# Rows that every partition needs, copied through DRAM by broadcast DMA in place of TensorE products, in a two-layer hybrid block with its delta-rule chain one step shorter

## What is computed

```
qkv = silu(conv(x @ w))                      # q, k, v: four heads each
q, k = l2_normalize(q), l2_normalize(k)      # one root per head and token
beta = sigmoid(ba)
g    = -exp(a_log) * softplus(aa + dt_bias)  # one number per head and token
gc   = cumsum(g) within a chunk
decay = exp(gc[i] - gc[j]) for j <= i
T    = inverse(I + strict_lower(beta k k^T * decay))
...                                          # scan over chunks with the state S
S    = S * exp(gc[last]) + (k * exp(gc[last] - gc))^T v_new
o    = rms_norm(o) * silu(z)                 # one root per head and token
```

## Time and profile before

| | us |
|---|---|
| median of 3 runs | 1946.79 (1946.22 to 1951.45) |
| the profiled execution | 1947.63 |
| its span in the profile | 1945.8 |
| PE busy | 1931.6 (99%) |
| DVE, ACT, POOL busy | 1021.6, 888.9, 851.3 |

### The profile page before, as it was taken

One profiled execution on the slowest core, in us unless ns is written; L12 is line 12 of the kernel. 1 busy time (PEld: TensorE's weight loads), 2 busy tenths in 40 slices (PEclk: granted clock), 3 DMA queues, 4 the chain that ended last, 5 costly groups with the idle time before them and its releaser, 6 DMA issues.

```text
span 1945.8 us, 23734 instructions
## 1 busy us (share of the span) xinstructions
PE 1931.6 (99%) x9108; PEld 1532.9 (79%) x9108; DVE 1021.6 (53%) x1832; ACT 888.9 (46%) x1355; POOL 851.3 (44%) x644
## 2 busy tenths in 40 slices
PE   9999999999999999999999999999999999999999
PEld 6878877877788878787877788677766788888887
DVE  5657755555745668666464747574644436101210
ACT  6455553344345455543344355586555444312321
POOL 4545432443445454422434445455322445444443
PEclk9999999999999999999999999999999999999999
DMA  5334542423535235632424545322111332222232
GB/s 202 128 110 135 139 137 73 162 76 118 187 107 175 90 114 147 162 109 71 153 65 141 189 154 162 136 76 98 65 56 55 119 107 89 98 97 98 98 114 71
DMA packets 94864, 227.69 MB, mean 117 GB/s; under 512 B 29880, under 2 KB 32952, under 8 KB 93440
## 3 DMA queue, kind: packets, MB, share of 16 engines
q1 hardware_dynamic: 89056, 223.03, 35.4%
q10 hardware_dynamic: 5696, 3.15, 0.6%
HBM read 194.01 MB, written 24.64 MB: 112 GB/s over the span
## 4 chain that ended last, share of the span: by engine, by line
PE 85%; DVE 7%; DMA 2%; ACT 2%; POOL 1%; SPq 1%; issue 1%; ACTq 0%; DVEq 0%
PE bank L442 84%; DVE ER L376 1%; DVE kv L376 1%; PE bank L446 1%; SPq L371 1%; POOL wl L376 1%; DMA X<-inverses 1%; DMA gt<-gates 1%; DVE scs L401 1%; DMA kv<-blocks 1%; DVE m8s L398 0%; ACT lt L428 0%; DVE lt L386 0%; DVE tmp L376 0%; ACT wh L431 0%
## 5 line engine op out<-in xcount | busy, mean ns | idle before, releaser
L376 POOL TENSOR_TENSOR wl<-st,wh 128x512 fp32r<-128x512 f32 x602 | 804.5, 1359 | 1019.3 <-ACT wh L431 1019.2
L442 PE MATMUL bank<-hh,wh 128*128 128x512 f32 x1616 | 651.8, 404 | 2.8 <-DVE hl L386 0.9
L442 PE MATMUL bank<-hh,wl 128*128 128x512 f32 x1616 | 629.8, 390 | 0.0
L442 PE MATMUL bank<-hl,wh 128*128 128x512 f32 x1616 | 629.3, 390 | 0.0
L431 ACT ACTIVATE wh<-st 128x1024 fp32r<-128x1024 f32 (+1 forms) x302 | 317.0, 1050 | 242.9 <-PE bank L442 194.5
L442 PEld LDWEIGHTS bank<-hh,wh 128*128 128x128 f32 x1616 | 303.4, 188 | 92.5 <-issue 24.6
L442 PEld LDWEIGHTS bank<-hl,wh 128*128 128x128 f32 x1616 | 303.6, 188 | 66.9 <-issue 6.9
L442 PEld LDWEIGHTS bank<-hh,wl 128*128 128x128 f32 x1616 | 303.3, 188 | 64.3
L376 DVE TENSOR_TENSOR xt<-xt,bank 128x512 f32<-128x512 f32 x40 | 27.5, 687 | 235.6 <-PE bank L442 235.6
L428 ACT ACTIVATE tmp<-bank 128x512 f32<-128x512 f32 x70 | 41.7, 596 | 156.8 <-PE bank L442 150.2
L442 PE MATMUL bank<-fh,wh 128*128 128x512 f32 x256 | 99.6, 389 | 0.0
(11 more groups left out here) (344 smaller groups left out, 2838.6 us busy)
## 6 DMA issues: line engine op xcount, KB each, us to landing
st<-units SPq DMA_DIRECT2D x300, 512.0 KB, 3.5
gates<-tmp SPq DMA_DIRECT2D x48, 256.0 KB, 2.8
gt<-gates SPq DMA_DIRECT2D x48, 256.0 KB, 3.7
pads<-tmp SPq DMA_DIRECT2D x32, 128.0 KB, 2.7
qk<-tmp SPq DMA_DIRECT2D x16, 256.0 KB, 4.3
x_scratch<-xt SPq DMA_DIRECT2D x2, 2048.0 KB, 8.7
xt<-x_scratch SPq DMA_DIRECT2D x2, 2048.0 KB, 8.3
ph<-phi SPq DMA_DIRECT2D x8, 512.0 KB, 4.6
```

Source lines behind the costliest of these rows:

```text
L376: return NOTHING if self.e is None else self.e.tensor_tensor(out, a, b, op)
L442: return NOTHING if self.e is None else self.e.matmul(out, lhsT, rhs, start=start, stop=stop, skip_group_check=share)
```

## The change

The products `spread`, `gl` and `G` are taken out. Each kind of row is now written to a DRAM tensor and read back by a DMA whose source has step 0 over 128 partitions (`everywhere`), so that all four heads' rows stand in every partition (1 MB per read). The head roots land in the tiles of aT and lT (L.qr, L.kr), the decays and the output roots in kv (L.G). DVE and ACT read these tiles in place of PSUM banks. PE's `delta` has 7 steps before the loop over heads where it had 8, and ACT, DVE and POOL one step fewer too; SP issues the new DMAs in its own `delta` and in the stretch before `pw`.

```
@@ shared tiles @@
+        L.G = kv
+        L.Gend = kv[:].rearrange("p h (b t) -> p b h t", t=128)[:, :, :, 127]
+        L.qr, L.kr = [t[:].rearrange("p h a b -> p h (a b)") for t in (L.aT, L.lT)]
@@ PE delta @@
             sums(5, L.aa4k, "dn", l, 1)
-            yield
-            yield
-            spread(aa4[0], "dn", l, 0)
-            yield
-            spread(aa4[1], "dn", l, 1)
-            yield
-            yield
+            yield from idle(4)
             o = bank(4, "tp", l)
             pe.wait_ge(*at("small_v", l, 4))
...
-            o = bank(5, "gl", l)
-            pe.mm(o[:, 0:16], ident[:, 127:128].broadcast_to([128, 128]), L.tpc[:, 0, :, :], True, True)
...
-                if n in (0, 2):
-                    pe.wait_ge(*at("rows", l))
-                    for m, q in ((n, Q4[1]), (n + 1, Q4[3])):
-                        pe.mm(bank(4 + m % 2, "G", l, m), ident[q, ...].broadcast_to([32, 128]), L.rw[q, :], True, True)
@@ PE front3 @@
-                if j == 2:
-                    spread(L.aa4[0], "on", l)
@@ ACT delta @@
-            yield from idle(6)
-            ac.wait_ge(*at("gl", l))
-            ac.act(L.egl[:].rearrange("p b c -> p (b c)"), banks[5][:, 0:16], ACT.Exp)
+            yield from idle(5)
+            ac.wait_ge(*at("decays", l, 1))
+            ac.act(L.egl[:], L.Gend, ACT.Exp)
@@ DVE delta, f = 0 (q) and 1 (k) @@
-                dv.wait_ge(*at("dn_up", l, f))
+                dv.wait_ge(*at(f"roots{f}", l, 1))
                 for c in range(4):
-                    dv.stt(x, x, 0.5 * ..., banks[4 + c][:], ALU.mult, ALU.mult)
+                    dv.stt(x, x, 0.5 * ..., (L.qr, L.kr)[f][:, c, :], ALU.mult, ALU.mult)
@@ SP @@
+        def everywhere(rows):
+            return rows.unsqueeze(0).broadcast_to([128, 4, T])
...
-            yield from idle(7)
+            yield from idle(2)
+            for f in range(2):
+                sp.wait_ge(*at("dn_r", l, f))
+                sp.dma(root_d[l, f], L.aa4[f][0:128:32, :])
+            for f in range(2):
+                sp.wait_ge(*at(f"roots{f}", l, 0))
+                sp.dma((L.qr, L.kr)[f], everywhere(root_d[l, f]))
+            yield from idle(2)
             sp.wait_ge(*at("small_v", l, 4))
-            sp.dma(L.rw[R3, :], L.rw[R1, :])
+            sp.dma(decay_d[l], L.rw[R1, :])
+            yield
+            sp.wait_ge(*at("decays", l, 0))
+            sp.dma(L.G[:], everywhere(decay_d[l]))
...
+            take(2)
+            sp.wait_ge(*at("on_r", l))
+            sp.dma(oroot_d[l], L.aa4[0][0:128:32, :])
+            take()
+            sp.wait_ge(*at("out_roots", l, 0))
+            sp.dma(L.G[:], everywhere(oroot_d[l]))
```

More of the change, by code:

```diff
@@ L285 @@
 SHARED = {
-    "pe_heads": "dn_mm tp gl h_g h_kk dn_up on_up h_w h_kv h_r h_uw sc_w sc_s sc_o on_mm",
+    "pe_heads": "dn_mm tp h_kk h_w h_kv h_r h_uw sc_w sc_s sc_o on_mm",
     "pe_rows": "norm_mm qk_mean q2_mm k2_mm pl_mm lru_mm",
@@ L550, in build @@
     cd_d = consts[:, n_cst:cpack.n]
+    root_d = nc.dram_tensor("roots", [2, 2, 4, T], F32).ap()
+    oroot_d = nc.dram_tensor("out_roots", [2, 4, T], F32).ap()
+    decay_d = nc.dram_tensor("decays", [2, 4, T], F32).ap()
     blk_d = nc.dram_tensor("blocks", [16, 4, 32, 32], F32).ap()
@@ L885, in sums @@
             t.then_inc(*sig(f"{name}_mm", *key))
[L887 to L892, removed]
         def delta(l):
@@ L1532, in delta @@
                     e = n % 2
[L1533 removed]
                     if n > 1:
                         ac.wait_ge(*at("h_qg", l, n - 2))
[L1536 to L1537 removed]
+                    ac.act(L.Y[e][:], L.G[:, n, :], ACT.Exp).then_inc(*sig("h_eg", l, n))
+                    ac.wait_ge(*at("h_gd", l, n))
                     ac.act(L.E[e][:], L.E[e][:], ACT.Exp).then_inc(*sig("h_dt", l, n))
@@ L2153, in delta @@
             yield
-            dv.wait_ge(*at("egl", l))
+            dv.wait_ge(*at("decays", l, 1))
             dv.wait_ge(*at("free4", "tp", l))
-            dv.tt(L.gcol[:, 1, :, :], f4(banks[5][:, 0:16]), gc, ALU.subtract).then_inc(*sig("free5", "gl", l))
+            dv.tt(L.gcol[:, 1, :, :], L.Gend, gc, ALU.subtract).then_inc(*sig("gend", l))
             dv.wait_ge(*at("gexp", l, 1))
@@ L2750, in delta @@
                 gp.set(a[:], 0.0).then_inc(*sig("x_zero", l, a is L.XT0))
-            yield from idle(8)
+            yield from idle(7)
             for n in range(5):
@@ L2863, in delta @@
             L = layer[l]
-            yield from idle(7)
-            sp.wait_ge(*at("small_v", l, 4))
-            sp.dma(L.rw[R3, :], L.rw[R1, :]).then_inc(*dma("rows", l))
-            yield from idle(3)
+            yield from idle(2)
+            for f in range(2):
+                sp.wait_ge(*at("dn_r", l, f))
+                sp.dma(root_d[l, f], L.aa4[f][0:128:32, :]).then_inc(*dma(f"roots{f}", l, 0))
+            for f in range(2):
+                sp.wait_ge(*at(f"roots{f}", l, 0))
+                sp.dma((L.qr, L.kr)[f], everywhere(root_d[l, f])).then_inc(*dma(f"roots{f}", l, 1))
+            yield from idle(2)
+            sp.wait_ge(*at("small_v", l, 4))
+            sp.dma(decay_d[l], L.rw[R1, :]).then_inc(*dma("decays", l, 0))
+            yield
+            sp.wait_ge(*at("decays", l, 0))
+            sp.dma(L.G[:], everywhere(decay_d[l])).then_inc(*dma("decays", l, 1))
+            yield from idle(4)
             for f in range(2):
@@ L2999, in sync_program @@
             weave(proj(l), (delta(l), RATES[0]))
-            take(4)
-            sp.wait_ge(*at("free7", "on_row", l, 3))
+            take(2)
+            sp.wait_ge(*at("on_r", l))
+            sp.dma(oroot_d[l], L.aa4[0][0:128:32, :]).then_inc(*dma("out_roots", l, 0))
+            take()
+            sp.wait_ge(*at("out_roots", l, 0))
+            sp.dma(L.G[:], everywhere(oroot_d[l])).then_inc(*dma("out_roots", l, 1))
+            take()
+            sp.wait_ge(*at("on_n", l, 3))
             sp.wait_ge(*at("sel", l, 3))
```

27 lines of the change are left out of this document (11 added, 16 removed).

## The result

The changed kernel takes 1982.35 us (median of 4 runs, 1981.22 to 1983.22) against 1947.05 for the kernel before in the same series: ratio 1.0171, 95% interval [1.0159, 1.0184], so 35 us slower. The forecast was 1953.4, with a range of 1944 to 1962: the sign was right, the size was not. The execution that was profiled has a span of 1980.1 us, 34.3 more than before.

What follows compares the result with a forecast made beforehand. PE was taken as the bound. Per layer, 9.0 us of wait at tp plus 1.5 of clock, less 6.3 of products and 0.9 of X waits, gave +3.3; both layers +6.6 on 1946.8: 1953.4 us, range 1944 to 1962.

Steps and rivals of the forecast that it cites:

- What bounds the kernel: PE, busy 1931.6 of 1945.8 us, is the bound nearly everywhere; every wait it gets is paid in full.
- What goes: Spreads (1.28 us each), products G and gl leave PE: 6.3 us per layer, 12.7 for both, none covered.
- Wait at tp, W + R = 9.0: PE waits before transposes tp for the scan: root write W 2.4 plus broadcast read R 6.6 us per layer, 5.6 to 11.3.
- Their operand in SBUF in place of PSUM changes nothing: DVE's multiplications, small rows and scan before tp still take 5.0 us when reading roots from SBUF.
- Clock, 1.5 us per layer: The long wait at tp may bring back a slow matmul stretch once per layer: 0 to 2.9 us, 1.5 taken.
- Decays and output roots hidden: Decays through DRAM have 3 us of cover at bank 0; output roots arrive about 353, read at 363.3, fully hidden.
- One step shorter: With delta's chain a step shorter, PE's waits for X<-inverses go: 0.9 us per layer gained, bounds 0 to 0.9.
- The states of the scan wait as before: PE's waits for the scan's states, 3.1 us in all, stay unchanged.
- The sum: Per layer 9.0 + 1.5 - 6.3 - 0.9 = +3.3 us, both +6.6: 1953.4 us, or 1954.2 for the profiled execution.
- much slower: Rival, 17 in 100: 128 reads of the same 8 KB crowd, R 8.6 or more; +6.5 us per layer, 1959.8.
- Faster: Rival, 8 in 100: no wait at tp, as g's rows need not stand behind late q; -7.2 per layer, 1932.4.
- Nothing: Rival, 33 in 100: R 5.1 and W 2.1 us, clock stays, so wait and savings cancel at 7.2; 1946.8.

Runs made afterwards that it cites:

- the filled run: The changed kernel with 32 products of no use in front of tp in each layer, filling the wait there: 1978.34 us, ratio 1.0151 to the kernel before.
- the plain read: The changed kernel with the broadcasts of q's and k's roots replaced by plain 1 MB reads of distinct weights: 1983.94 us, one run.
- the run with the scan first: The changed kernel with the rows of g and their scan ahead of q's multiplications on DVE: 1972.47 us, ratio 1.0101 to the kernel before.

## Why the prediction was wrong, by its own steps

- **What bounds the kernel**: right. The new waits on PE (31.2 us) stand in full in the span, and the clock came on top.
- **What goes**: right where it could be taken alone. For the output roots the measured interval (1.6 to 5.3 us) holds the 2.6. The sum of 12.7 was not measured in one piece.
- **Wait at tp, W + R = 9.0**: 8.2 us in both layers. The number is right by luck, in offsetting errors. W was 1.7 (below the bound of 2.1) and R 4.9 (6.6 taken; the lower bound was 3.5), and DVE's part 7.1 for 5.0; SP and PE were 0.9 and 0.5 us early. The Trainium skill, page "DMA: Bandwidth & Descriptors", section "Anatomy of one DMA", would give 2.0 and 4.4 as estimates: nearer to these two durations than my rows, though the page gives that fit for DMAs that GpSimd issues, and these are SP's. My reason for 6.6, the twin behind the read, did not hold: it was there, and R was 4.9.
- **"Their operand in SBUF in place of PSUM changes nothing"**: wrong in detail. Four steps of the decay matrix, 128x128 each, took 3.18 us in the changed kernel where POOL was reading and 1.1 where it was not; with the operand in PSUM all four groups took 1.13 (16 records: 4.5 us before, 6.5 after), also while POOL worked. DVE's timeline in the changed kernel:

```profile
154.04 3.18 DVE L386 SCALAR_TENSOR_TENSOR ER<-kv,tpc,cst 128x128 f32<-128x128 f32 x4
...
159.25 1.14 DVE L386 SCALAR_TENSOR_TENSOR ER<-kv,tpc,cst 128x128 f32<-128x128 f32 x4
```

and POOL's:

```profile
154.18 2.63 POOL L376 TENSOR_TENSOR wl<-st,wh 128x512 fp32r<-128x512 f32 x2 [0.92 <-ACT wh L431]
```

DVE's and POOL's of the kernel before, at the second head:

```profile
148.76 1.13 DVE L386 SCALAR_TENSOR_TENSOR ER<-bank,tpc,cst 128x128 f32<-128x128 f32 x4 [0.66 <-ACT Y L428]
```

```profile
148.32 2.53 POOL L376 TENSOR_TENSOR wl<-st,wh 128x512 fp32r<-128x512 f32 x2 [5.04 <-ACT wh L431]
```

The Trainium skill, page "SBUF — State Buffer", section "Who interferes with whom", has the rule: a DVE instruction with two inputs in SBUF and a GpSimd instruction that reads SBUF exclude each other. The trace agrees: 3.18 us against 1.13. In the changed kernel about 1.1 us of the wait at tp belong here: q's multiplications took 3.56 us with POOL at work from 129.90, and 2.48 before, with POOL at work too but the roots in PSUM. In the four runs that copy the decays with the step in place and no edit to the scan or to tp, the second head's four instructions take 3.2 us and PE waits 1.3 us per layer for DVE aT; where TensorE spreads the decays this wait is absent. It takes back 2.6 of the 5 us that copying the decays was to bring.
- **Clock, 1.5 us per layer**: right at tp, 2.0 (the filled run). But there were more slow stretches than the one that I counted (behind nr and the tail of the scan, 0.50 too): over the whole kernel nearly 16 us where 3.0 were in the sum, about half a microsecond for each one of waiting.
- **Decays and output roots hidden**: right for PE in the changed kernel, with the price above once the step is back. ACT's egl stood directly behind the gate's rows at 144.44 and did not hold a bank; yA had no wait.
- **"One step shorter" costs nothing and brings 0.9 us**: this is the step that failed. It cost about 23 us (30.8 by putting it back, less 7.7 that PE then waits less at tp). The 0.9 us per layer for X<-inverses did go, as forecast, but 17.7 us of other waits came. I looked at one reader of the inverse, X, and took for granted that whoever makes it is a step earlier too. PE comes to all the chain's products a step earlier; the inverse comes 5.0 us later, 2.4 of them because SP's blocks had come to stand behind a unit load (moving them alone gave 13.6 us back) and 2.6 because the inversion itself took longer. DVE, 9.5 of 10 us busy for 50 us, could not catch up. "The states of the scan wait as before" was wrong too: X from 3.1 to 4.7 us and scs 3.1, as I read it because nothing is left on PE to stand between the last selection products.
- **The sum**: the profiled execution lies 27.7 us above its forecast of 1954.2. The new later waits are 17.7 of that, the clock 12.8 more than forecast, the wait at tp 1.6 less, and small waits 1.2 less.
- **The rivals**: "much slower" named crowded reads; the plain read shows none. "Faster", by freeing the scan from q: the runs show that it moves the wait to the decay matrix. "Nothing" is the nearest to the truth for the copies alone (1.0016). None of the rivals had the shorter chain as its mechanism, though the change says it in its own description.

## What to carry to other kernels

A step taken out of a chain that is interleaved with other work shortens it only if every queue in it can follow: compare the new order on each queue, the DMA queue above all (here the blocks slid behind a load that waits), look for the stretch in which the engine off the bound is full (here DVE at 9.5 of 10 us) and can't make up for a late start, and count what stood in each DMA's travel time as filler. Price a wait of PE with the slow stretch behind it, here 1.25 to 1.7 times its length, and price each part of a change with and without the others before adding them up. Rows copied through DRAM paid off where their reader is late anyway (output roots; k's roots with the decays, by 0.2 to 0.5%), not where a chain begins with them (q's roots).

## What the runs showed of the hardware

- A broadcast read of 8 KB to 128 partitions (1 MB written) was there 4.9 us after its issue in the changed kernel and 4.2 in the run with the scan first, a plain read of 1 MB of distinct data 5.0 (one run).
- In a wait of 8.2 us the granted clock fell to 0.50 before the wait was over and stayed there for another 4 us of full work; with dummy products in the wait it stayed at 1.00.
- The same four instructions of DVE with two tile operands took 3.18 us while POOL worked, and 4.96 in the run with the scan first, once an operand had moved from PSUM to SBUF; 1.14 while POOL did not work, and 1.13 with the operand in PSUM even while it did.
